# First attention with three row buffers, and scores three rounds ahead of the turn on TensorE

## What is computed

```python
logit_s = jnp.einsum('bqghd,bqgkd->bqghk', qt, ks).astype(jnp.float32) + bias_s
logit_s = jnp.where(valid_s[:, :, :, None, :], logit_s, NEG_INF)
p_s = jax.nn.softmax(logit_s, axis=-1)
o_s = jnp.einsum('bqghk,bqgkd->bqghd', p_s.astype(vs.dtype), vs)
...
o = gt[..., 0:1] * o_c + gt[..., 1:2] * o_s + gt[..., 2:3] * o_w
```

## Time and profile before

| | us |
|---|---|
| median of 3 runs | 2400.56 |
| lowest, highest | 2398.49, 2400.91 |
| the profiled execution, its own time | 2397.24 |
| its span, first to last instruction | 2395.3 |

### The profile page before, as it was taken

How to read it: one execution, slowest core, us unless ns; L and a number is a source line. 1 busy time by engine, 2 the same in 40 slices (tenths; PEclk the granted TensorE clock), 3 DMA queues, 4 the chain that set the end, 5 groups by cost and what they waited for, 6 DMA issues and landing times.

```text
span 2395.3 us, 35731 instructions
## 1 busy us (share of the span) xinstructions
PE 2361.5 (99%) x14579; PEld 2052.4 (86%) x14579; DVE 1474.6 (62%) x2592; ACT 877.2 (37%) x1390; POOL 183.1 (8%) x259
## 2 busy tenths in 40 slices
PE   9999999999999999999999999999999999999998
PEld 7888888888886678888889999999999999998997
DVE  6555344355557645444468987887666656883784
ACT  4123222233457732212244772774333333212212
POOL 0000000000037610000001200210100000000000
PEclk9999999999999999999999999999999999999999
DMA  5236233324342212222223532542222222223223
GB/s 174 88 102 149 88 103 127 123 92 131 113 130 59 62 58 101 88 101 92 88 88 109 131 80 93 121 108 87 90 78 76 68 89 89 90 103 123 89 91 120
DMA packets 67622, 239.13 MB, mean 100 GB/s; under 512 B 22482, under 2 KB 33170, under 8 KB 43634
## 3 DMA queue, kind: packets, MB, share of 16 engines
q1 hardware_dynamic: 31044, 200.14, 24.6%
q0 software_dynamic: 5952, 18.44, 4.2%
q10 hardware_dynamic: 30496, 18.73, 3.5%
HBM read 228.41 MB, written 10.09 MB: 100 GB/s over the span
## 4 chain that ended last, share of the span: by engine, by line
PE 86%; DVE 7%; POOL 2%; issue 2%; ACT 1%; DMA 1%; SPq 0%; DVEq 0%; POOLq 0%; ACTq 0%
PE ps L1146 43%; PE ps L1440 25%; PE ps L1730 5%; PE ps L1551 3%; POOL Sb L541 2%; DVE wlo L1785 1%; PE ps L1659 1%; PE ps L1387 1%; PE ps L1369 1%; PE ps L1273 1%; PE ps L1633 1%; DMA raw<-in_stream 1%; PE ps L1314 1%; PE ps L1502 0%; DVE Y L2301 0%
## 5 line engine op out<-in xcount | busy, mean ns | idle before, releaser
L638 ACT ACTIVATE whi<-raw 128x2048 fp32r<-128x2048 f32 (+2 forms) x185 | 345.7, 1869 | 855.8 <-PE ps L1146 451.8
L1785 DVE TENSOR_TENSOR wlo<-raw,whi 128x2048 fp32r<-128x2048 f32 (+3 forms) x210 | 417.4, 1988 | 72.7 <-ACT whi L638 72.5
L1146 PE MATMUL ps<-parts,whi 128*128 128x512 f32 x1328 | 418.2, 396 | 1.2 <-DVE ct L1927 1.2
L1440 PE MATMUL ps<-parts,whi 128*128 128x258 f32 (+1 forms) x2400 | 403.1, 290 | 1.1 <-issue 0.8
L1440 PEld LDWEIGHTS ps<-parts,whi 128*128 128x128 f32 x2400 | 331.0, 189 | 11.4 <-issue 10.0
L1146 PEld LDWEIGHTS ps<-parts,whi 128*128 128x128 f32 x1328 | 248.3, 188 | 62.5 <-issue 3.8
L1146 PE MATMUL ps<-parts,wlo 128*128 128x512 f32 x664 | 262.6, 395 | 0.0
L1440 PE MATMUL ps<-parts,wlo 128*128 128x258 f32 (+1 forms) x1200 | 242.4, 284 | 0.0
L1146 PE MATMUL ps<-Mlo,whi 128*128 128x512 f32 x512 | 203.0, 396 | 0.0
L1146 PE MATMUL ps<-Mhi,whi 128*128 128x512 f32 x512 | 203.0, 396 | 0.0
L1146 PE MATMUL ps<-Mhi,wlo 128*128 128x512 f32 x512 | 203.0, 396 | 0.0
(11 more groups left out here) (419 smaller groups left out, 3937.1 us busy)
## 6 DMA issues: line engine op xcount, KB each, us to landing
raw<-in_stream SPq DMA_DIRECT2D x186, 1024.0 KB, 4.8
csb<-sums_d POOLq DMA_DIRECT2D x16, 512.0 KB, 6.1
bands<-scratch ACTq DMA_DIRECT2D x7, 1024.0 KB
csf<-sums_d POOLq DMA_DIRECT2D x32, 128.0 KB, 6.2
tabs<-bands ACTq DMA_DIRECT2D x8, 418.0 KB, 4.3
X<-in_x SPq DMA_DIRECT2D x4, 512.0 KB, 6.9
near_a<-bands ACTq DMA_DIRECT2D x8, 256.0 KB, 2.7
Q_odd<-parts POOLq DMA_DIRECT2D x8, 256.0 KB, 4.4
```

Of the source, the lines that this page charges most:

```text
L638: nc.scalar.activation(whi[:, s, 0:cols], raw[:, s, 0:cols], ACT.Copy).then_inc(hi_done, 1)
L1146: mm = nc.tensor.matmul(out, w[:, s, at], x(k), start=k + j == 0, stop=k == k_tiles - 1 and j == 2)
L1440: mm = nc.tensor.matmul(ps[:, 2 * par + h, 0:w], wt[:, s, at], x[:, k, a + h * w:a + (h + 1) * w], start=k + j == 0, stop=k == k_tiles - 1 ...
L1785: low = nc.vector.tensor_tensor(wlo[:, s, a:b], raw[:, s, a:b], whi[:, s, a:b].bitcast(F32), ALU.subtract)
```

## The change

The third buffer is memory that already exists: `acc` and `sq` become two views of one tensor `acc_sq`, and its first 1280 columns are the rows of rounds with n % 3 = 2. `nmax` and `rsum` get a third slot. Every engine works one round further ahead: VectorE takes the reciprocal of round n + 2 and the score rows of n + 3 in its iteration n, and ScalarE the exponentials of n + 3. On TensorE `scores(n + 3)` stands ahead of `turn(n)`. POOL stages the queries in r = 6 and 7 instead of r = 7 and 0, behind a wait for all scores of the old group. The diff, with `n % 2` to `n % 3` shown at one place of each kind:

```diff
-        acc = sb("acc", [P, TOK])
-        sq = sb("sq", [P, 2, TOK])
+        acc_sq = sb("acc_sq", [P, 3, TOK])
+        acc, sq = acc_sq[:, 0, :], acc_sq[:, 1:3, :]
...
-            Sb = sb("Sb", [P, 2, SPAN], F32, scope)
+            Sb2 = sb("Sb", [P, 2, SPAN], F32, scope)
+            Sb = (Sb2[:, 0, :], Sb2[:, 1, :], acc_sq[:, :, :].rearrange("p a n -> p (a n)")[:, 0:SPAN])
...
-            nmax = sb("nmax", [P, 2, QT], F32, scope)
-            rsum = sb("rsum", [P, 2, QT], F32, scope)
+            nmax = sb("nmax", [P, 3, QT], F32, scope)
+            rsum = sb("rsum", [P, 3, QT], F32, scope)
...
-                    row = Sb[:, n % 2, first(t):first(t + 1)]
+                    row = Sb[n % 3][:, first(t):first(t + 1)]
...
-                if r == ROUNDS - 1 and g + 2 < GROUPS:
-                    pool.wait_ge(s_full, n + 1)
-                    stage_queries(pool, g + 2, q_staged[g % 2], (0,))
+                if r >= ROUNDS - 2 and g + 2 < GROUPS:
+                    pool.wait_ge(s_full, ROUNDS * (g + 1))
+                    stage_queries(pool, g + 2, q_staged[g % 2], (r - ROUNDS + 2,))
                 if to < GROUPS:
                     if 0 < r < 5:
                         pool.wait_ge(probs_ready, 4 * (n + 1))
-                    if r == 0 and g:
-                        stage_queries(pool, to, q_staged[to % 2], (1,))
...
             exps(1)
+            exps(2)
             for n in range(ALL_ROUNDS):
...
-                if n + 2 < ALL_ROUNDS:
-                    exps(n + 2)
+                if n + 3 < ALL_ROUNDS:
+                    exps(n + 3)
...
             scores(1)
+            scores(2)
             pe.wait_ge(cmp_ready, 2)
             for n in range(ALL_ROUNDS):
+                if n + 3 < ALL_ROUNDS:
+                    scores(n + 3)
                 turn(n)
-                if n + 2 < ALL_ROUNDS:
-                    scores(n + 2)
                 beside_round(n)
...
             compressed_sums(0)
+            sums(1)
+            scores(2)
             for n in range(ALL_ROUNDS):
                 g, r = divmod(n, ROUNDS)
                 last = g == GROUPS - 1
                 turned(n)
-                if n + 1 < ALL_ROUNDS:
-                    sums(n + 1)
                 if n + 2 < ALL_ROUNDS:
-                    scores(n + 2)
+                    sums(n + 2)
+                if n + 3 < ALL_ROUNDS:
+                    scores(n + 3)
```

More of the change, by code:

```diff
@@ L538, in weighed @@
                 for t in range(QT):
-                    row = Sb[:, n % 2, first(t):first(t + 1)]
+                    row = Sb[n % 3][:, first(t):first(t + 1)]
                     at = 3 * (g * HPG + h) + 1 + branch
-                    nc.gpsimd.tensor_scalar(row, row, rsum[:, n % 2, t:t + 1], gates[:, t, at:at + 1], ALU.mult, ALU.mult).then_inc(probs_ready, 1)
+                    nc.gpsimd.tensor_scalar(row, row, rsum[:, n % 3, t:t + 1], gates[:, t, at:at + 1], ALU.mult, ALU.mult).then_inc(probs_ready, 1)
             def compressed_weighed(g):
@@ L890, in exps @@
                     act.wait_ge(ttr_done, 4 * n + t + 1)
-                    row = Sb[:, n % 2, first(t):first(t + 1)]
-                    nc.scalar.activation(row, row, ACT.Exp, bias=nmax[:, n % 2, t:t + 1], scale=-1.0,
-                                         accum_out=rsum[:, n % 2, t:t + 1]).then_inc(exp_done, 1)
+                    row = Sb[n % 3][:, first(t):first(t + 1)]
+                    nc.scalar.activation(row, row, ACT.Exp, bias=nmax[:, n % 3, t:t + 1], scale=-1.0,
+                                         accum_out=rsum[:, n % 3, t:t + 1]).then_inc(exp_done, 1)
                 g, h, branch = of_round(n)
@@ L1368, in turn @@
                         bank, at = turn_at(t, k)
-                        mm = nc.tensor.transpose(ps[:, bank, at:at + P], Sb[:, n % 2, first(t) + k * P:first(t) + (k + 1) * P], ident)
+                        mm = nc.tensor.transpose(ps[:, bank, at:at + P], Sb[n % 3][:, first(t) + k * P:first(t) + (k + 1) * P], ident)
                 mm.then_inc(pt_full, 1)
@@ L2042, in scores @@
                     w = (t + 1) * P
-                    nc.vector.tensor_tensor_reduce(Sb[:, n % 2, first(t):first(t) + w], ps[:, bank, at:at + w], near_of(h)[:, SEQ - w:SEQ],
-                                                   -1.0, -2 * MASKED, ALU.add, ALU.min, nmax[:, n % 2, t:t + 1]).then_inc(ttr_done, 1)
+                    nc.vector.tensor_tensor_reduce(Sb[n % 3][:, first(t):first(t) + w], ps[:, bank, at:at + w], near_of(h)[:, SEQ - w:SEQ],
+                                                   -1.0, -2 * MASKED, ALU.add, ALU.min, nmax[:, n % 3, t:t + 1]).then_inc(ttr_done, 1)
             def sums(n):
                 dve.wait_ge(exp_done, 4 * n + 4)
-                nc.vector.reciprocal(rsum[:, n % 2, :], rsum[:, n % 2, :]).then_inc(sums_ready, 1)
+                nc.vector.reciprocal(rsum[:, n % 3, :], rsum[:, n % 3, :]).then_inc(sums_ready, 1)
             def turned(n):
```

## The result

| | before | after |
|---|---|---|
| median | 2400.73 us (4 runs) | 2436.2 us (4 runs) |
| lowest, highest | 2398.49, 2401.19 | 2433.3, 2439.3 |
| the profiled execution's span | 2395.3 | 2433.9 |
| mean granted clock of it | 0.999 | 0.990 |
| first row of the output projection | 855.88 | 894.53 |

The changed kernel takes 1.0144 times as long [1.0128, 1.016], 35.5 us more. The forecast was 2421 us with a range up to 2431: the sign was right, and the time lies 5 us above the range. The span of before is that of the earlier trace rows; its median is taken with one more run than the table ahead of the prediction.

The account below looks back on a forecast made before the run. The old attention loop was taken as bound by POOL's weighing between VectorE's reciprocal and TensorE's turn. Rounds +20.9, start +4.8 and tail -4.7 gave +21.0 us, on the median 2400.56 about 2421 us, range 2412 to 2431.

Parts of the forecast that it names:

- what the third buffer does: Attention rounds: POOL's weighing done at 3.3 us after a turn, two rounds ahead, so POOL leaves the loop; alone a gain.
- The rule on bubbles: Gaps before nearly every second turn: consistent bubbles can mean too few buffers, so the extra buffer would make the kernel faster.
- the ring: Attention loop: turn, VectorE's copy, reciprocal and score rows, next scores, next turn wait on each other; +20.9 us over 28 rounds.
- an even interval: Attention loop, interval beginning with an even round: copy, score rows, scores and turn in sequence, 5.20 us, 14 times.
- odd ones: Attention loop, intervals behind odd rounds: TensorE's values work outlasts VectorE's 2.52 us, giving 5.67 to 5.79 us.
- the start: Attention's beginning: extra sums and scores precede the first copy, moving it from 706.86 to 711.62, +4.8 us.
- the tail: After round 28's turn: no scores left and weighing done early, 12.1 us against 16.8 us, -4.7 us.
- rival 4: Attention: TensorE's clock falls from idling about 2.3 us in half the rounds; +78 us at most, a few if seldom; chance 0.03.
- Rival 2: Attention loop: rounds cost only about 4.7 us as before, so no change that can be told, 2400 us; chance 0.03.

Follow-up runs that it names:

- turn_first: The changed kernel with three row buffers, but TensorE's old order, turn(n) ahead of scores(n+3): 2389.99 us, ratio 0.9947 against the kernel before.
- order_only: The kernel before, two row buffers kept, with only scores(n+2) moved ahead of turn(n) on TensorE: 2442.21 us, ratio 1.0158.
- after_fine: The changed kernel with TensorE's scores waiting for each PSUM bank separately instead of once for all of the last round: 2409.53 us, ratio 1.0042 against before.
- after_fill: The changed kernel plus eight unused 256-column matmuls behind the turn of each even round: 2422.71 us, ratio 1.0079 against the kernel before.
- after_again: The changed kernel, unchanged, run once more: 2434.66 us, ratio 1.0135 against the kernel before.
- after_start_fill: The changed kernel plus one unused 256-column matmul in each of 16 steps of the last compression product: 2436.54 us, ratio 1.0146 against before.
- order_fill: order_only plus eight unused matmuls behind the turn of each even round, as in after_fill: 2423.53 us, ratio 1.0097 against the kernel before.
- before_again: The kernel before, unchanged, timed and traced once more: 2401.97 us over 10 executions, ratio 1.0004.

## Why the prediction was wrong in size

**Right: what the third buffer does.** It takes POOL out of the loop (no wait of the turn left), and with the old order it is a gain, 11.5 us in turn_first. The rule on bubbles that the prediction cites from the Trainium skill, page "Perfetto Trace Analysis", section "Identifying Performance Opportunities", holds here for the buffer with the old order and not for the whole change: the order of TensorE's steps brought a new gap, which hangs on PSUM banks that were not multiplied.

**Right: the ring.** Forecast 5.20 us for an even interval and 5.67 to 5.79 for odd ones, measured 5.15 and 5.62 to 5.73. The 28 rounds were put at 153.2 us; undisturbed ones sum to 151.7. The scores wait 16 times, 2.2 us each, as said. order_only shows that it comes from the order, after_fine that it hangs on VectorE's last reads.

**Right, as far as it can be told apart: the start as a path.** +4.8 us forecast. The trace has +15.0, with TensorE at 1.2 GHz almost throughout: the last compression product is read at 701.58 against 697.97, and scores and turn take 2.72 and 2.33 us in place of 1.54 and 1.31. The 10.2 us put down to the clock are what is left when the forecast's 4.8 is taken off, not a measurement. The nearest measurement is after_fill, which has no long fall and is at 1.2 GHz from about 705.8 to 712.7:

```profile
705.12 2.13 PE L1315 MATMUL ps<-K_even,Q_even 128*128 128x128 f32 x8 [1.97 <-DVE nmax L2058]
...
709.17 2.69 PE L1315 MATMUL ps<-K_even,Q_even 128*128 128x128 f32 x8 [1.92 <-DVE nmax L2058]
```

These are scores(2) and scores(3), forecast at 705.40 and 708.90. The first copy there is at 713.44, 1.8 us behind the forecast of 711.62, with scores(3) and turn(0) slowed by the clock.

**Slightly off: the tail.** -4.7 forecast, -3.7 measured. Compressed values of round 29 wait 0.94 us for VectorE, which makes the low part of a head pair (L2090) between its score rows and the next copy. At the other rounds that work fits in VectorE's wait, as forecast; in the tail, where a round takes only 2.95 us, it does not.

**The step that failed is rival 4.** The prediction saw that TensorE would idle about 2.3 us in half the rounds, and had one row on what the clock does behind a gap: 1.51 us, once, at 1.00. From that it gave a fall 3 in 100 and left it out of the range, although it wrote itself that for 2.3 us the rows say nothing. A cost with no row should have had a real chance, and its "few microseconds" a place at the upper end. What the runs showed in its place: 44 us at 1.2 GHz in the trace of the changed kernel, of which the falls in the rounds cost 7.9 us and the one at the start about 10. The Trainium skill, page "TensorE: Matmul & The Clock Gate", section "Why this matters for your kernels", warns of idle gaps between bursts of matmuls. The runs agree with it in direction and not in length: its row speaks of gaps longer than any wait measured here, and waits of 1.7 to 2.6 us were enough. In numbers:

| kernel | waits of the scores for VectorE | us at 1.2 GHz: start, rounds | median |
|---|---|---|---|
| after | 2.2 us each | 27, 17 | 2436.2 |
| after_again, the same kernel | 2.2 us each | 27, 31 | 2434.7 |
| after_start_fill | 2.1 us each | 7, 34 | 2436.5 |
| order_only | 2.2 us each | 24, 34 | 2442.2 |
| after_fill | 1.3 us each, the fillers in front | 7, 3 | 2422.7 |
| order_fill | as after_fill | 3, 0, and 3 behind round 28 | 2423.5 |
| after_fine | 1.1 us each | 7, 0 | 2409.5 |
| turn_first | 13 waits of 0.7 us | 3, 0 | 2390.0 |

The account of the trace is then: ring +19.4, start +4.8 by its path, clock +10.2 at the start and +7.9 in the rounds, tail -3.7: +38.6 us. The two terms of the start were measured only as their sum. Without the clock it is +20.5, and the forecast was +21.0; that these are so close is partly luck, since the rounds came out 1.5 us shorter than forecast and the tail 1.0 us longer. The clock's price is 7.9/17=0.46 us for each microsecond at 1.2 GHz in the rounds and by the split above 10.2/27.3=0.37 at the start; the medians give 0.4 (from after_fill to the changed kernel 34 us more at 1.2 GHz in the traces and 13.5 us more time). It is under a half where part of the time passes in waits for VectorE (1.97 and 1.92 us at the start), which no clock of TensorE makes longer.

**Smaller slips in the working.** The terms named for the range give 2414 to 2428 on 2421.6, and the range was written as 2413 to 2429; the result lies outside either. Rival 2's 0.65 and 0.4 us a round come to 14.7 us and not to the 21 that no change would need. Rival 4's "at most" of 78 us counts scores and turns only, and leaves out the values.

**Open.** The long fall begins at about 694.5 us, in the last compression product, ahead of every instruction that the change moved, and with TensorE busy all the time in the records (4.75 of 4.75 us from 690 on). It stands in both traces of the changed kernel and in that of order_only, and in none of the others. after_fill and after_fine don't have it, although their edits all lie behind it, so neither the order of the rounds by itself nor those edits can be shown to decide it. Nor is it shown to belong to the new order: 13 of 45 executions of the kernel before have, by their mean clock, about as much low clock (before_again), and so have single executions of after_fine (2416.97 us at 0.993) and order_fill (2430.12 us at 0.992). About 10 of the 35.5 us may then be a fall that comes by chance in any of these kernels; eight executions of the changed one, all low in clock, speak against pure chance, but only two were traced. That gaps bring the short falls is shown as far as three different ways of shortening them (fillers, finer waits, the other order) leave 0 to 3 us of 17 to 34; why five of the fourteen even rounds pay, and not the others, stays open.

## What to carry to other kernels

An added buffer and the order that uses it are two changes: ask of each what the next step waits for, and look for resources that were not multiplied with it (here single PSUM banks, given back only by VectorE's last read). When a forecast gives TensorE a new idle time in every other round, put a fall of the clock into the range, with the cost of the nearest measured case, even if the trace of before shows none. Look at the mean clock of every execution and not only of the profiled one. Wait for PSUM bank by bank: it gave 27 us with the scores first, 11 of them in the intervals themselves and the others with the clock, and 8 us with the turn first.

## What the runs showed of the hardware

- Waits of TensorE of 1.7 to 2.6 us, 14 of them in 28 rounds, came with five to seven stretches at 1.2 GHz, of about 3.4 or 6.8 us each (after, after_again, order_only, after_start_fill); with waits of 1.1 us there were none in the rounds (after_fine). Eight matmuls without use, about 1 us in each pair of rounds of 10.8 us, left 3.4 us of the 17 to 31 us at 1.2 GHz in the rounds (after_fill).
- A microsecond at 1.2 GHz cost 0.46 us in the rounds, and about 0.4 us in the medians.
- A fall of 24 to 27 us began with TensorE busy in every record before it, in three of thirteen traces.
- The executions of one kernel differ by its clock: before at 2397 to 2403 us with 0.996 to 0.999, and 2408 with 0.993; the changed one 2431 to 2444 with 0.992 to 0.986.
